# Prompt attention with a third pair of probability buffers

## The chip, the cores and the metric
One core of a Trainium2 chip runs the whole program: one decoder layer for a prompt of 1024 tokens and for 8 sequences of 4 new tokens each. The metric is the device time of one execution in microseconds (us). Engines: PE is TensorE (PEld its weight loads), DVE is VectorE, ACT is ScalarE, POOL is GpSimd, SP is SyncE, which issues most DMAs. Every engine has a queue of its own; what one needs of another it waits for by semaphore.

## The reference, cut to what matters
The layer normalises, projects, runs attention beside a gated convolution, projects out, and then runs a mixture of experts and a gated embedding. The part that the change touches is the attention of the prompt. For each of 8 heads it mixes three dilation patterns, weighted by their softmax denominators, which is one softmax over all keys with a bias that counts each distance as often as a pattern holds it:

```
s   = einsum('bdnqhc,bdnkhc->bdnhqk', qb, kb) * HEAD_DIM**-0.5 + bias
s   = where(valid, s, NEG)
mx  = max(s);  e = exp(s - mx);  den = sum(e)
num = einsum('bdnhqk,bdnkhc->bdnqhc', e, vb)
...
wts = exp(mxs - max(mxs))
out = sum(wts * nums) / sum(wts * dens)
```

The kernel computes for each head and each block of 128 queries the scores against all earlier keys, adds a bias table that holds the log of the counts and the mask, and takes one softmax.

## The kernel before, in words
All arithmetic is float32. In the prompt attention two heads make a pair (four pairs), and each pair takes eight steps, one for each block i of 128 query rows, in the order i = 7, 0, 6, 1, 5, 2, 4, 3 (STEPS, line 139). Step i has 128 (i + 1) keys, so heavy and light steps alternate. In what follows n counts all 32 steps and hh is the head of the pair.

A step passes through these operations. PE: `score(n)` (line 1552), both heads, into PSUM banks 0 to 3, one group of banks for each head, so the next score waits until both were read. DVE: `bias(n, hh)` (L1092) adds the table Z to the scores, writes the result to the probability buffer E and its negated maximum to `nmax`. ACT: `exp(n, hh)` (L796), in place, with its sum in `den`. DVE: `normalise(n, hh)` (L1099 the reciprocal, L1101 the scaling in place). PE: `trans_p(n)` (L1566) turns the i + 1 blocks of each head with the identity, up to four blocks to a PSUM bank, with two banks (4 and 5) in turn; a bank is used again once ACT has copied it out. ACT: `evac_pt(n, hh)` (L807) does that copy into the buffer PTb, of which there are two pairs. PE: `weigh(n)` (L1579) multiplies the values V with the turned probabilities into bank 6 or 7. DVE: `evac_o(n)` (L1106) copies the output to aT. When all eight steps of a pair have been copied, POOL squares, sums and scales that pair's output (lines 615 to 621). E has two pairs of buffers, used by turns; `bias(n)` waits until the transposes of step n - 2 have read theirs.

The order on each engine is written out by hand. PE: score(n), trans_p(n-1), weigh(n-2). ACT: evac_pt(n-1, 0), exp(n, 0), evac_pt(n-1, 1), exp(n, 1). DVE: bias(n, 0), bias(n, 1), evac_o(n-3), normalise(n, 0), normalise(n, 1). SP loads the next pairs' tables Z after counts of the semaphore `scored`, and the first caches for the sample attention after the last one. The sample attention begins on PE, ACT and DVE behind the last step of this stage; its later loads wait for semaphores that hang on the stage's end.

Of the kernel before, what the change touches and what calls it, by code (L numbers as in the profile page):

```python
# [26 lines left out]
ALU = mybir.AluOpType  # L27
ACT = mybir.ActivationFunctionType
AX = mybir.AxisListType

P = 128
D = 1024
SEQ = 1024
# [106 lines left out]
NSTEP = len(STEPS)  # L140


def tp_uses(n):

    return sum(2 * -(-(i + 1) // 4) for _, i in STEPS[:n])
# [37 lines left out]
def build(nc, I, O):  # L183
    ctx = ExitStack()
    with ctx, nc.allow_non_contiguous_dma(reason="gains and router weights, a few KB"):
        _build(nc, I, O, ctx)


def _build(nc, I, O, ctx):
    sem_cache = {}  # L190

    def S(name):
        if name not in sem_cache:
            sem_cache[name] = ctx.enter_context(nc.semaphore(name))
        return sem_cache[name]

    def sb(name, n, dt=F32):
        return ctx.enter_context(nc.sbuf_tensor(name, [P, n], dt))
# [8 lines left out]
    def view(region, at, *dims):  # L207
        n = int(np.prod(dims))
        v = region[:, at:at + n]
        if len(dims) == 2:  # L210
            v = v.rearrange("p (a b) -> p a b", a=dims[0])
        if len(dims) == 3:
            v = v.rearrange("p (a b c) -> p a b c", a=dims[0], b=dims[1])
        return v

    ident = sb("ident", P)
# [12 lines left out]
    small = sb("small", 320)  # L229
    qts = view(sb("qts", NG * SAMP), 0, NG, SAMP)  # L230
    kts = view(sb("kts", NG * SAMP), 0, NG, SAMP)
    R1 = sb("R1", 26880)
    R2 = sb("R2", 12880)
    R3 = sb("R3", 4224)
    R4 = sb("R4", 6144)
# [31 lines left out]
    a_sum = view(R1, 13312, SEQ)  # L267
    Z = [view(R1, 16384 + 1024 * s, SEQ) for s in range(4)]
    aT = view(R1, 22656, CC, TOK)
    E = [[view(R4, 2048 * p + 1024 * hh, SEQ) for hh in range(2)] for p in range(2)]  # L270
    PTb = [[view(r, at + 1024 * hh, PT, P) for hh in range(2)] for r, at in ((R4, 4096), (R1, 20480))]

    near = [view(r, at, NG, NEAR) for r, at in ((R2, 0), (R2, 3584), (R2, 8192), (R1, 20480))]
# [67 lines left out]

    ssx, ms_x, rs_x = small[:, 0:2], small[:, 2:4], small[:, 4:6]
    hd_s, hd_r, hd_q = small[:, 6:22], small[:, 22:38], small[:, 38:54]
    nmax, den, rden = small[:, 54:58], small[:, 58:62], small[:, 62:66]
    ssc, rc = small[:, 88:97], small[:, 97:106]
    nms, dens, rdens = small[:, 106:107], small[:, 107:108], small[:, 108:109]
    ssa, ra = small[:, 140:149], small[:, 150:159]
# [5 lines left out]
    bank = [ctx.enter_context(nc.psum_tensor(f"pair{i}", [P, 1024], F32)) for i in range(4)]  # L353
    bk = [bank[i // 2][:, 512 * (i % 2):512 * (i % 2) + 512] for i in range(8)]
# [353 lines left out]
    def _(act):  # L708
# [82 lines left out]

        def exp(n, hh):
            w = P * (STEPS[n][1] + 1)
            k = 2 * (n % 2) + hh
            act.wait_ge(S("scored"), 2 * n + hh + 1)
            act.activation(E[n % 2][hh][:, 0:w], E[n % 2][hh][:, 0:w], ACT.Exp, bias=nmax[:, k:k + 1],  # L796
                           scale=-1.0, accum_out=den[:, k:k + 1]).then_inc(S("exp_done"), 1)

        def evac_pt(n, hh):
            i = STEPS[n][1]  # L800
            use = tp_uses(n) + hh * (-(-(i + 1) // 4))
            if n >= 2:
                act.wait_ge(S("ot_full"), n - 1)
            for j0 in range(0, i + 1, 4):
                m = min(4, i + 1 - j0)
                act.wait_ge(S("tp_full"), use + 1)
                act.activation(PTb[n % 2][hh][:, j0:j0 + m, :], bk[4 + use % 2].rearrange("p (a b) -> p a b", b=P)[:, 0:m, ::-1],  # L807
                               ACT.Copy).then_inc(S("tp_free"), 1)
                use += 1

        act.wait_ge(S("new_out"), 32)
        for n in range(NSTEP):
            if n >= 1:
                evac_pt(n - 1, 0)
            exp(n, 0)
            if n >= 1:
                evac_pt(n - 1, 1)
            exp(n, 1)
        evac_pt(NSTEP - 1, 0)
        evac_pt(NSTEP - 1, 1)  # L820


        def evac_near(b):
# [140 lines left out]
    def _(dve):  # L964
# [62 lines left out]
        for q in range(CC):  # L1027
# [23 lines left out]
            for j in range(3):  # L1051
                w = wj[:, j, q:q + 1]
# [31 lines left out]
        def bias(n, hh):  # L1084
            pair, i = STEPS[n]
            w = P * (i + 1)
            k = 2 * (n % 2) + hh
            dve.wait_ge(S(f"w_in{2 * (pair % 2) + hh}"), W_DONE[2 * (pair % 2) + hh] + 16 * (pair // 2 + 1))
            dve.wait_ge(S("s_full"), 2 * n + hh + 1)
            if n >= 2:  # L1090
                dve.wait_ge(S("tp_full"), tp_uses(n - 1))
            dve.tensor_tensor_reduce(E[n % 2][hh][:, 0:w], bank[hh][:, 0:w], Z[2 * (pair % 2) + hh][:, SEQ - w:SEQ], -1.0, 3e38,  # L1092
                                     ALU.add, ALU.min, nmax[:, k:k + 1]).then_inc(S("scored"), 1)

        def normalise(n, hh):
            w = P * (STEPS[n][1] + 1)
            k = 2 * (n % 2) + hh
            dve.wait_ge(S("exp_done"), 2 * n + hh + 1)
            dve.reciprocal(rden[:, k:k + 1], den[:, k:k + 1]).then_inc(S("rden"), 1)  # L1099
            dve.wait_ge(S("rden"), 2 * n + hh + 1)  # L1100
            dve.tensor_scalar(E[n % 2][hh][:, 0:w], E[n % 2][hh][:, 0:w], rden[:, k:k + 1], None, ALU.mult).then_inc(S("p_ready"), 1)  # L1101

        def evac_o(n):
            pair, i = STEPS[n]
            dve.wait_ge(S("ot_full"), n + 1)
            dve.tensor_copy(aT[:, pair, P * i:P * i + P], bk[6 + n % 2][:, 0:P]).then_inc(S("ot_free"), 1)  # L1106

        for n in range(NSTEP):
            bias(n, 0)
            bias(n, 1)  # L1110
            if n >= 3:
                evac_o(n - 3)
            normalise(n, 0)
            normalise(n, 1)
        for n in range(NSTEP - 3, NSTEP):
            evac_o(n)


# [310 lines left out]
    def _(pe):  # L1429
# [9 lines left out]
        for q in range(CC):  # L1439
            last = pe.transpose(bk[7][:, 16 * q:16 * q + 16], st_in[:, P * q:P * q + P], ident[0:16, 0:16])  # L1440
# [68 lines left out]
        for q in range(CC):  # L1509
            pe.wait_ge(S(f"kv_in{q % 2}"), 16 * (q // 2 + 1))  # L1510
            for j, (lo, n) in enumerate(PIECES):
                use = 3 * q + j
                for which, full, b in ((2, "cC_full", use % 2), (0, "ch_full", 2 + use % 2), (1, "cB_full", 4 + j)):
# [10 lines left out]
                    for c in range(DC):  # L1524
                        last = mm(bk[b][:, 0:n], wB[q % 2][:, c, which, :], xT[:, c, lo:lo + n], start=(c == 0), stop=(c == DC - 1))  # L1525
# [3 lines left out]
        for q in range(CC):  # L1529
            last = pe.transpose(bk[0][0:18, P * q:P * q + P], u_new[:, 18 * q:18 * q + 18], ident[:, :])  # L1530
        last.then_inc(S("new_full"), 1)
        pe.wait_ge(S("y_sum"), CC)
        for t in range(TILES):
            n = P if t < PT else SAMP
            last = mm(bk[7][0:n, t:t + 1], y_sum[:, P * t:P * t + n], ones[:, 0:1], start=True, stop=True)
# [7 lines left out]
        def score(n):  # L1543
            pair, i = STEPS[n]
            w = P * (i + 1)
            if n >= 1:
                pe.wait_ge(S("scored"), 2 * n)
            for c0 in range(0, w, 512):
                m = min(512, w - c0)
                for hh in range(2):  # L1550
                    half = slice(64 * hh, 64 * hh + 64)
                    last = mm(bank[hh][:, c0:c0 + m], QT[half, pair, P * i:P * i + P], KT[half, pair, c0:c0 + m], start=True, stop=True)  # L1552
                    if c0 + m == w:
                        last.then_inc(S("s_full"), 1)

        def trans_p(n):
            i = STEPS[n][1]
            use = tp_uses(n)
            for hh in range(2):
                pe.wait_ge(S("p_ready"), 2 * n + hh + 1)  # L1560
                for j0 in range(0, i + 1, 4):
                    m = min(4, i + 1 - j0)
                    if use >= 2:
                        pe.wait_ge(S("tp_free"), use - 1)
                    for j in range(m):
                        last = pe.transpose(bk[4 + use % 2][:, P * j:P * j + P], E[n % 2][hh][:, P * (j0 + j):P * (j0 + j) + P], ident[:, :])  # L1566
                    last.then_inc(S("tp_full"), 1)
                    use += 1

        def weigh(n):  # L1570
            pair, i = STEPS[n]
            pe.wait_ge(S("tp_free"), tp_uses(n + 1))
            if n >= 2:
                pe.wait_ge(S("ot_free"), n - 1)
            for j in range(i + 1):
                for hh in range(2):
                    half = slice(64 * hh, 64 * hh + 64)
                    c = DH * (2 * pair + hh)
                    last = mm(bk[6 + n % 2][half, 0:P], V[:, j, c:c + DH], PTb[n % 2][hh][:, j, :], start=(j == 0), stop=(j == i))  # L1579
            last.then_inc(S("ot_full"), 1)  # L1580

        for n in range(NSTEP):
            score(n)
            if n >= 1:
                trans_p(n - 1)
            if n >= 2:
                weigh(n - 2)
        trans_p(NSTEP - 1)
        weigh(NSTEP - 2)
        weigh(NSTEP - 1)  # L1590
# [77 lines left out]
        for t in range(PT):  # L1668
            last = mm(bk[7][:, t:t + 1], a_sum[:, P * t:P * t + P], ones[:, 0:1], start=True, stop=True)
# [18 lines left out]
        for q in range(CC):  # L1688
            last = mm(bk[4][0:SAMP, 0:1], as_sq[:, q, :], ones[:, 0:1], start=(q == 0), stop=(q == CC - 1))
# [230 lines left out]
```

## Time and profile before
| | |
|---|---|
| median of 3 runs | 1448.4 us (1447.89 to 1451.6) |
| profiled execution | 1454.46 us, its span 1452.4 us |
| PE busy, share of the span | 1262.4 us, 87% |
| DVE, ACT, POOL busy | 403.7, 320.8, 168.5 us |
| granted TensorE clock, mean of the span | 0.931 |
| prompt attention, 403.5 to 556 us | PE busy 126.03, DVE 107.31, ACT 95.55 of 152.50 us, clock 0.90 |

The busy time says how much of the span an engine worked, the chain of waits says which work ended last, and the timeline gives each instruction's start and length. The granted clock is 1.00 at 2.4 GHz and 0.50 at 1.2 GHz. The start of one instruction to the start of the next is the better price of PE's work, since the ends of matmuls are modelled.

### The profile page before, as it was taken

Reading aid. Unit: us, or ns where it says so; the run is one execution under the profiler, and the core shown is the slowest. Engines: PE = TensorE matmul, PEld = TensorE weight load, DVE = VectorE, ACT = ScalarE, POOL = GpSimd, SP = SyncE. Lnnn points to the kernel's source line nnn. Section 1 sums busy time; section 2 is a strip of 40 time slices with the busy share of each in tenths; the row PEclk is TensorE's granted clock in tenths of the full one; section 3 lists DMA queues with packets and bytes.
Section 4 is the critical chain, followed back from the end, with each engine's and each line's share of the span. In section 5 each row is a group of like instructions: output and inputs, shape, how many; then the busy total and the mean of one; then the engine's idle time right before and its main releaser. Section 6 shows DMA issues by size and latency. Waiting matters only on the chain.

```text
span 1452.4 us, 16889 instructions
## 1 busy us (share of the span) xinstructions
PE 1262.4 (87%) x6484; PEld 816.4 (56%) x6484; DVE 403.7 (28%) x829; ACT 320.8 (22%) x625; POOL 168.5 (12%) x222
## 2 busy tenths in 40 slices
PE   4999999999978887567999407999999999789995
PEld 1444445666555557243555307888888888534442
DVE  1121221122257775121322531111111111033332
ACT  2132321000057664130111200111111111123332
POOL 0000000000031221000000052222222221100000
PEclk9999999999979998787999758999999999979998
DMA  7111400130040005898111422888888888432210
GB/s 260 36 51 43 119 15 19 44 102 0 27 127 31 30 1 162 202 267 301 73 73 47 191 89 64 308 308 294 310 297 322 317 318 327 189 129 90 86 50 33
DMA packets 64453, 208.84 MB, mean 144 GB/s; under 512 B 16158, under 2 KB 29758, under 8 KB 48528
## 3 DMA queue, kind: packets, MB, share of 16 engines
q1 hardware_dynamic: 50704, 177.61, 35.6%
q0 software_dynamic: 13696, 30.49, 5.8%
q8 instruction: 37, 0.61, 0.2%
q14 instruction: 16, 0.13, 0.0%
HBM read 194.43 MB, written 29.89 MB: 154 GB/s over the span
## 4 chain that ended last, share of the span: by engine, by line
PE 81%; DMA 6%; DVE 6%; issue 3%; ACT 2%; POOL 1%; SPq 1%; POOLq 0%; ACTq 0%; DVEq 0%
PE pair L1778 17%; PE pair L1473 12%; PE pair L1525 11%; PE pair L1710 8%; PE pair L1877 8%; PE pair L1788 8%; DMA R<-in_cache_v 4%; PE pair L1552 3%; PE pair L1566 2%; PE pair L1769 2%; PE pair L1859 2%; PE pair L1579 2%; DVE R L1101 1%; PE pair L1603 1%; POOL list_dram L640 1%
## 5 line engine op out<-in xcount | busy, mean ns | idle before, releaser
L1778 PEld LDWEIGHTS pair<-R 128*128 128x128 f32 x2048 | 247.6, 197 | 16.5 <-issue 14.2
L1778 PE MATMUL pair<-R 128*128 128x128 f32 x2048 | 247.9, 282 | 1.7 <-DVE R L1357 1.7
L1525 PE MATMUL pair<-R 128*128 128x352 f32 x576 | 172.5, 463 | 0.4 <-ACT kts L758 0.4
L1473 PE MATMUL pair<-R 128*128 128x512 f32 x384 | 170.6, 601 | 0.8 <-DVE R L993 0.8
L1525 PEld LDWEIGHTS pair<-R 128*128 128x128 f32 x576 | 110.2, 192 | 61.8 <-issue 1.4
L1473 PEld LDWEIGHTS pair<-R 128*128 128x128 f32 x384 | 72.9, 193 | 87.8 <-issue 86.6
L1788 PE MATMUL pair<-R,bias_s 128*128 128x512 f32 x256 | 115.3, 593 | 1.4 <-DVE bias_s L1363 1.4
L1710 PE MATMUL pair<-R 128*128 128x512 f32 x256 | 114.6, 602 | 0.0
L1877 PE MATMUL pair<-R 128*128 128x512 f32 x256 | 112.9, 599 | 0.8 <-ACT R L932 0.8
L1357 DVE COPY R<-pair 128x512 f32<-128x512 f32 x64 | 41.3, 686 | 238.2 <-PE pair L1769 238.2
L1877 PEld LDWEIGHTS pair<-R 128*128 128x128 f32 x256 | 49.2, 193 | 62.9 <-issue 62.9
L898 ACT ACTIVATE R<-pair 128x512 f32<-128x512 f32 x32 | 19.1, 597 | 292.4 <-PE pair L1788 292.4
L1710 PEld LDWEIGHTS pair<-R 128*128 128x128 f32 x256 | 48.3, 193 | 55.6 <-issue 55.6
L1769 PE MATMUL pair<-ident,R 128*128 128x128 f32 x256 | 34.3, 278 | 45.8 <-DMA R<-m_dram,idx_c 45.8
L1788 PEld LDWEIGHTS pair<-R,bias_s 128*128 128x128 f32 x256 | 46.2, 190 | 48.2 <-issue 45.9
L1566 PE MATMUL pair<-ident,R 128*128 128x128 f32 x288 | 46.3, 302 | 22.1 <-DVE R L1101 16.2
L1769 PEld LDWEIGHTS pair<-ident,R 128*128 128x128 f32 x256 | 31.5, 189 | 46.6 <-issue 46.6
L1566 PEld LDWEIGHTS pair<-ident,R 128*128 128x128 f32 x288 | 34.0, 151 | 40.6 <-DVE R L1101 36.2
L807 ACT ACTIVATE R<-pair 128x512 f32<-128x512 f32 (+3 forms) x96 | 43.8, 484 | 43.3 <-PE pair L1566 43.0
L796 ACT ACTIVATE R<-R,small 128x1024 f32<-128x1024 f32 (+7 forms) x64 | 49.4, 772 | 6.0 <-DVE small L1092 5.5
L1092 DVE CUSTOM_DVE_ANT_0 R<-pair,R 128x1024 f32<-128x1024 f32 (+7 forms) x64 | 45.8, 753 | 13.8 <-PE pair L1552 13.7
L1552 PE MATMUL pair<-R 64*128 64x512 f32 (+3 forms) x192 | 44.6, 573 | 4.1 <-DVE small L1092 3.5
(266 smaller groups left out, 1172.0 us busy)
## 6 DMA issues: line engine op xcount, KB each, us to landing
R<-in_w_gate SPq DMA_DIRECT2D x32, 1024.0 KB, 7.3
R<-in_w_up SPq DMA_DIRECT2D x32, 1024.0 KB, 9.7
R<-in_w_down SPq DMA_DIRECT2D x32, 1024.0 KB, 12.9
R<-in_x_prompt SPq DMA_DIRECT2D x16, 512.0 KB, 3.5
R<-in_cache_k SPq DMA_DIRECT2D x8, 1024.0 KB, 7.8
R<-in_cache_v SPq DMA_DIRECT2D x8, 1024.0 KB, 19.7
R<-y_dram SPq DMA_DIRECT2D x16, 512.0 KB, 4.3
R<-in_w_in SPq DMA_DIRECT2D x3, 2048.0 KB, 10.3
```

The costliest lines, as they stand in the source:

```text
L796: act.activation(E[n % 2][hh][:, 0:w], E[n % 2][hh][:, 0:w], ACT.Exp, bias=nmax[:, k:k + 1], scale=-1.0, accum_out=den[:, k:k + 1]).then_i ...
L807: act.activation(PTb[n % 2][hh][:, j0:j0 + m, :], bk[4 + use % 2].rearrange("p (a b) -> p a b", b=P)[:, 0:m, ::-1], ACT.Copy).then_inc(S(" ...
L1092: dve.tensor_tensor_reduce(E[n % 2][hh][:, 0:w], bank[hh][:, 0:w], Z[2 * (pair % 2) + hh][:, SEQ - w:SEQ], -1.0, 3e38, ALU.add, ALU.min, n ...
L1473: last = mm(bk[4 + part][0:n, :], xTs[a.u][:, c, 0:n], wA[:, c, AD * part:AD * part + AD], start=(c == 0), stop=(c == DC - 1))
L1525: last = mm(bk[b][:, 0:n], wB[q % 2][:, c, which, :], xT[:, c, lo:lo + n], start=(c == 0), stop=(c == DC - 1))
L1552: last = mm(bank[hh][:, c0:c0 + m], QT[half, pair, P * i:P * i + P], KT[half, pair, c0:c0 + m], start=True, stop=True)
L1566: last = pe.transpose(bk[4 + use % 2][:, P * j:P * j + P], E[n % 2][hh][:, P * (j0 + j):P * (j0 + j) + P], ident[:, :])
L1710: last = mm(bk[2 * pair + j][0:n, :], lhs[:, q, P * a.t:P * a.t + P], w_out[:, c0 + q, 512 * j:512 * j + 512], start=(q == 0), stop=(q == ...
L1769: last = pe.transpose(bk[j][:, CAP * (c % 4):CAP * (c % 4) + CAP], xg[u][:, c:D:DC], ident[0:CAP, 0:CAP])
L1778: last = mm(bk[2 + u][:, CAP * (2 * side + j):CAP * (2 * side + j) + CAP], w[:, c, j:FE:2], xgT[u][:, c, :], start=(c == 0), stop=(c == DC ...
L1788: last = mm(bk[4 + 2 * u + j][0:CAP, :], hT[u][:, q, :], wd[s][:, q, 512 * j:512 * j + 512], start=(q == 0), stop=(q == 1))
L1877: last = mm(bk[2 + j][0:n, :], hnT[a.u][:, c, 0:n], w_pg[c][:, 512 * j:512 * j + 512], start=(c == 0), stop=(c == DC - 1))
```

## The change
A third pair of buffers for E is placed in region R1 at 14336, `nmax`, `den` and `rden` have six columns instead of four, and E is used by n % 3. PE transposes step n - 2 and weighs step n - 3 behind score(n). ACT runs exp(n, 0), evac_pt(n-2, 0), exp(n, 1), evac_pt(n-2, 1). DVE runs both bias operations of n, then the scaling of n - 1, then the output copy of n - 4. `bias(n)` waits for the transposes of step n - 3. The buffers PTb and all PSUM banks stay as they were.

```diff
-    E = [[view(R4, 2048 * p + 1024 * hh, SEQ) for hh in range(2)] for p in range(2)]
+    E = [[view(r, at + 1024 * hh, SEQ) for hh in range(2)] for r, at in ((R4, 0), (R4, 2048), (R1, 14336))]
...
-    nmax, den, rden = small[:, 54:58], small[:, 58:62], small[:, 62:66]
+    nmax, den, rden = small[:, 54:60], small[:, 60:66], small[:, 66:72]
...
         act.wait_ge(S("new_out"), 32)
         for n in range(NSTEP):
-            if n >= 1:
-                evac_pt(n - 1, 0)
             exp(n, 0)
-            if n >= 1:
-                evac_pt(n - 1, 1)
+            if n >= 2:
+                evac_pt(n - 2, 0)
             exp(n, 1)
-        evac_pt(NSTEP - 1, 0)
-        evac_pt(NSTEP - 1, 1)
+            if n >= 2:
+                evac_pt(n - 2, 1)
+        for n in range(NSTEP - 2, NSTEP):
+            evac_pt(n, 0)
+            evac_pt(n, 1)
...
-            if n >= 2:
-                dve.wait_ge(S("tp_full"), tp_uses(n - 1))
+            if n >= 3:
+                dve.wait_ge(S("tp_full"), tp_uses(n - 2))
...
             bias(n, 0)
             bias(n, 1)
-            if n >= 3:
-                evac_o(n - 3)
-            normalise(n, 0)
-            normalise(n, 1)
-        for n in range(NSTEP - 3, NSTEP):
+            if n >= 1:
+                normalise(n - 1, 0)
+                normalise(n - 1, 1)
+            if n >= 4:
+                evac_o(n - 4)
+        normalise(NSTEP - 1, 0)
+        normalise(NSTEP - 1, 1)
+        for n in range(NSTEP - 4, NSTEP):
             evac_o(n)
...
             score(n)
-            if n >= 1:
-                trans_p(n - 1)
             if n >= 2:
-                weigh(n - 2)
+                trans_p(n - 2)
+            if n >= 3:
+                weigh(n - 3)
+        trans_p(NSTEP - 2)
+        weigh(NSTEP - 3)
         trans_p(NSTEP - 1)
         weigh(NSTEP - 2)
         weigh(NSTEP - 1)
```
The remaining lines of the diff put n % 3 for n % 2 where E, `nmax`, `den` and `rden` are indexed.

## Rows read from the trace of the kernel before

**Rows 1.** Windows: us, PE, PEld, DVE, ACT, POOL busy, granted clock, DMA share, GB/s
```profile
487.00:524.00 37.00, 31.29 (x270) 21.07 (x268) 27.19 (x73) 23.28 (x56) 7.60 (x3) 0.91 0.01 1
```

**Rows 2.** Chain that ended last, in order: start us, us, what
```profile
441.43 1.97 PE pair L1552 x8
...
475.29 1.97 PE pair L1552 x8
...
512.19 1.97 PE pair L1552 x8
...
545.38 1.06 PE pair L1552 x4
...
553.65 0.29 DVE R L1106
```

**Rows 3.** Who waited for whom, 419 to 553 us: total us, times, longest
```profile
PEld pair L1566 <- DVE R L1101: 33.0, 35, 2.4
```

**Rows 4.** Timeline from step i = 6: start, us, instruction, idle before and its releaser
```profile
450.68 1.77 PE L1552 MATMUL pair<-R 64*128 64x512 f32 x8
...
452.38 0.44 PE L1566 MATMUL pair<-ident,R 128*128 128x128 f32 x2
452.58 1.10 DVE L1092 CUSTOM_DVE_ANT_0 R<-pair,R 128x896 f32<-128x896 f32 x1 [1.21 <-PE pair L1552]
452.75 1.73 PEld L1579 LDWEIGHTS pair<-R 128*64 128x64 f32 x32 [0.17 <-issue]
...
453.72 1.04 ACT L796 ACTIVATE R<-R,small 128x896 f32<-128x896 f32 x1 [0.63 <-DVE small L1092]
...
454.76 0.26 ACT L807 ACTIVATE R<-pair 128x128 f32<-128x128 f32 x1
```

**Rows 5.** Timeline: an evacuation and the transposes that it lets go
```profile
424.30 0.98 ACT L807 ACTIVATE R<-pair 128x512 f32<-128x512 f32 x2 [0.54 <-PE pair L1566]
...
425.04 0.96 PE L1566 MATMUL pair<-ident,R 128*128 128x128 f32 x7 [0.51 <-ACT R L807]
```

**Rows 6.** Timeline of the steps with i = 4 and i = 7
```profile
433.78 1.35 PE L1552 MATMUL pair<-R 64*128 64x512 f32 x8
...
435.06 0.88 PE L1566 MATMUL pair<-ident,R 128*128 128x128 f32 x6
...
436.95 0.47 ACT L807 ACTIVATE R<-pair 128x384 f32<-128x384 f32 x1
...
441.36 1.99 PE L1552 MATMUL pair<-R 64*128 64x512 f32 x8
...
443.27 1.09 PE L1566 MATMUL pair<-ident,R 128*128 128x128 f32 x8
...
445.88 0.58 ACT L807 ACTIVATE R<-pair 128x512 f32<-128x512 f32 x1
```

**Rows 7.** Timeline: the score of step 1
```profile
409.94 0.80 PE L1552 MATMUL pair<-R 64*128 64x128 f32 x4 [2.59 <-DVE small L1092]
```

**Rows 8.** Timeline: POOL's work for a pair and the scaling beside it
```profile
454.98 1.89 POOL L615 TENSOR_TENSOR R<-R 128x1024 f32<-128x1024 f32 x1 [41.89 <-DVE R L1106]
455.08 2.27 DVE L1101 TENSOR_SCALAR R<-R,small 128x896 f32<-128x896 f32 x1
...
457.46 1.36 DVE L1101 TENSOR_SCALAR R<-R,small 128x896 f32<-128x896 f32 x1
...
491.32 2.59 DVE L1101 TENSOR_SCALAR R<-R,small 128x896 f32<-128x896 f32 x1
```

**Rows 9.** Timeline of PE's pauses; windows of PE: us, busy, granted clock
```profile
457.41 0.98 PE L1566 MATMUL pair<-ident,R 128*128 128x128 f32 x7 [1.96 <-DVE R L1101]
...
528.17 1.37 PE L1566 MATMUL pair<-ident,R 128*128 128x128 f32 x7 [1.96 <-DVE R L1101]
...
491.00:491.10 0.10, 0.00 (x0) 0.89 0.00 0
497.90:498.00 0.10, 0.10 (x2) 0.98 0.00 0
```

More of the change, by code:

```diff
@@ L793, in exp @@
             w = P * (STEPS[n][1] + 1)
-            k = 2 * (n % 2) + hh
+            k = 2 * (n % 3) + hh
             act.wait_ge(S("scored"), 2 * n + hh + 1)
-            act.activation(E[n % 2][hh][:, 0:w], E[n % 2][hh][:, 0:w], ACT.Exp, bias=nmax[:, k:k + 1],
+            act.activation(E[n % 3][hh][:, 0:w], E[n % 3][hh][:, 0:w], ACT.Exp, bias=nmax[:, k:k + 1],
                            scale=-1.0, accum_out=den[:, k:k + 1]).then_inc(S("exp_done"), 1)
@@ L1086, in bias @@
             w = P * (i + 1)
-            k = 2 * (n % 2) + hh
+            k = 2 * (n % 3) + hh
             dve.wait_ge(S(f"w_in{2 * (pair % 2) + hh}"), W_DONE[2 * (pair % 2) + hh] + 16 * (pair // 2 + 1))
             dve.wait_ge(S("s_full"), 2 * n + hh + 1)
-            if n >= 2:
-                dve.wait_ge(S("tp_full"), tp_uses(n - 1))
-            dve.tensor_tensor_reduce(E[n % 2][hh][:, 0:w], bank[hh][:, 0:w], Z[2 * (pair % 2) + hh][:, SEQ - w:SEQ], -1.0, 3e38,
+            if n >= 3:
+                dve.wait_ge(S("tp_full"), tp_uses(n - 2))
+            dve.tensor_tensor_reduce(E[n % 3][hh][:, 0:w], bank[hh][:, 0:w], Z[2 * (pair % 2) + hh][:, SEQ - w:SEQ], -1.0, 3e38,
                                      ALU.add, ALU.min, nmax[:, k:k + 1]).then_inc(S("scored"), 1)
@@ L1096, in normalise @@
             w = P * (STEPS[n][1] + 1)
-            k = 2 * (n % 2) + hh
+            k = 2 * (n % 3) + hh
             dve.wait_ge(S("exp_done"), 2 * n + hh + 1)
@@ L1100, in normalise @@
             dve.wait_ge(S("rden"), 2 * n + hh + 1)
-            dve.tensor_scalar(E[n % 2][hh][:, 0:w], E[n % 2][hh][:, 0:w], rden[:, k:k + 1], None, ALU.mult).then_inc(S("p_ready"), 1)
+            dve.tensor_scalar(E[n % 3][hh][:, 0:w], E[n % 3][hh][:, 0:w], rden[:, k:k + 1], None, ALU.mult).then_inc(S("p_ready"), 1)
         def evac_o(n):
@@ L1565, in trans_p @@
                     for j in range(m):
-                        last = pe.transpose(bk[4 + use % 2][:, P * j:P * j + P], E[n % 2][hh][:, P * (j0 + j):P * (j0 + j) + P], ident[:, :])
+                        last = pe.transpose(bk[4 + use % 2][:, P * j:P * j + P], E[n % 3][hh][:, P * (j0 + j):P * (j0 + j) + P], ident[:, :])
                     last.then_inc(S("tp_full"), 1)
```

## The prediction

> **What bounds the kernel now.** I read the stage's windows first, then the chain that ended last, then who waited for whom, then the timeline of single steps. The windows show that the stage belongs to PE: in a 37 us stretch PE is busy for 31.3 us [rows 1], DVE and ACT for less. The chain gives the period of a head pair (eight steps): the 128-row blocks i = 7, 0, 6, 1, 5, 2, 4, 3. It passes the first score of pairs 1, 2 and 3 at 441.43, 475.29 and 512.19 us, the last score at 545.38 and the last output copy at 553.65 [rows 2]. So the periods are 33.86 and 36.90 us, and the stage, which begins at about 403.5, takes 150 us. In the waits the largest one of PE in this stage is for the scaling of the probabilities (L1101): 33.0 us over 35 times on the weight-load side [rows 3]. That is the wait which the change aims at: a transpose stands one step behind its score, and the step's exp and scaling are not done when PE comes to it. After the stage the sample attention waits for its end by the same semaphores as before, so whatever the stage gains or loses I take to the end of the kernel one for one.
>
> **The change, part by part.** With a distance of two steps every p_ready is long there: the scaling of step n-2 ends before PE has finished step n-1. This removes the waits of rows 3. What is late next is the question, and it is in ACT's order. Before: evacuate first half of n-1, exp(n,0), evacuate second half, exp(n,1). After: exp(n,0), evacuate first half of n-2, exp(n,1), evacuate second half. The transposes use two PSUM banks (up to four blocks each), and every half of a step with i of 4 or more fills both. So the second half's first transpose needs an evacuation that now stands behind exp(n,0), which needs bias(n,0), which needs the score that PE has only just made. And because heavy (i = 7, 6, 5, 4) and light steps alternate, n and n-2 are both heavy: before, the heavy transposes stood beside a light exp.
>
> Price of that wait, from the step with i = 6: score starts 450.68, bias 452.58, exp 453.72, ACT free for the next one 454.76 [rows 4], that is 4.08 us after the score began. From the start of an evacuation to the transpose that it lets go is 0.74 us (424.30 to 425.04) [rows 5]. So PE can start the second half 4.82 us into the step. It gets there earlier: score 1.70 us (to 452.38) [rows 4] and eight transposes at 0.107 us (0.86 for eight, the busy 1.09 of rows 6 being modelled past its hand-over) make 2.56. Pause: 2.26 us. In the same way i = 7: 4.52 + 0.74 = 5.26 against 1.91 + 0.54 (the block it turns is i = 4 of the pair before, five transposes) = 2.45, pause 2.81; i = 4: 3.17 + 0.74 = 3.91 against 1.28 + 0.64 = 1.92, pause 1.99 [rows 6]; i = 5 lies between: 4.36 against 2.24, pause 2.12. Together 9.2 us of pauses in each pair. The light steps have none: one bank for each half, both free by then.
>
> PE's own work in a pair: 72 transposes at 0.107 and 8 hand-overs of 0.17 are 9.0 us; 144 weighting matmuls at 0.054 (1.73 us for 32) [rows 4] and 8 hand-overs are 9.1; the scores are 1.91 + 1.70 + 1.49 + 1.28 for the heavy and about 2.9 for the light ones, 9.3. Sum 27.4 us, with the pauses 36.6. Against that the before has 33.86 and 36.90 [rows 2]: 6.5 and 9.5 above the same work. The longer of the two holds things that I price below.
>
> What the change saves beside rows 3: when a pair ends, GpSimd squares and scales its output (454.98), and the scaling on DVE takes 2.27 us beside it and 2.59 in the later pairs, where GpSimd has one more multiply, against 1.36 for the same shape only partly beside it [rows 8]. PE waits for both. Afterwards GpSimd starts some 5 us later in the pair, at the output copy which now follows the scaling, and what it blocks is a light step's scaling that PE needs a step later: hidden, at most 2.6 us a pair if the cover were gone. The bias operation itself ran at its usual length beside GpSimd.
>
> Start and end. Before, the third score stood behind the first step's transposes. It can now start once bias(1) is done: score 1 runs from 409.94 for 0.80 us [rows 7], then 0.2, two short biases and 0.14, so at 411.6. Steps 2 to 7 are then scores of 7.0, 1.7 more for the first of them at the lower clock, transposes of steps 0 to 5 of 6.7, weightings of steps 0 to 4 of 6.0 and three pauses of 6.4: 27.8, so the next pair begins at 439.4 instead of 441.43: -2.1 us. Pairs 1 to 3 up to the last score: 3 x 36.6 less the last step's 3.3 (score 1.06, transposes 0.81, weighting 1.46) = 106.5 against 545.38 - 441.43 = 103.95: +2.5. After the last score one more transpose step and one more weighting are left (2.3 us of work), less 0.9 of the 1.6 us that PE now waits in those 8.27: +1.4. The wider nmax/den/rden, the third buffer's place and the queue of SP (its table loads wait for counts of scored, as before) cost nothing; that engine idles here. Sum without the clock: -2.1 + 2.5 + 1.4 = +1.8 us.
>
> **The clock.** PE's pauses of 1.96 us, three in this stage (the first and the last in rows 9), came from the blocked scaling. The first left the granted clock at 2.4 GHz, the other two were each followed by 1.2 GHz, the middle one from 491.1 to 497.9, that is 6.8 us [rows 9]. A spell costs at least what the two periods differ by, less the longer second scaling: 3.04 - (2.59 - 1.36) = 1.8 us [rows 2, 8]; at most half of 6.8, 3.4 us, if PE has no pause in it to hide behind. After the change there are 15 pauses of 1.99 to 2.81 us (three in pair 0, four in each other), each at least as long as those that tipped the clock two times in three. I take six in ten: 9 spells, at 2.2 us, nearer the measured price: 20 us. (The two spells of before are in its periods already, and its 1.96 us pauses are gone.) Bounds: none, 0, and all at the high price, 51.
>
> Forecast: +1.8 + 20 = +22 us on the profiled execution's 1454.5. That execution is 6 us above the median of 1448.4; I put the difference on the median: 1470 us.
>
> **A rule of the skill.** The trace shows ACT's exp and evacuations in program order only, in every step of rows 4 to 6. The Trainium skill, page "TensorE: Matmul & The Clock Gate", section on the architectural detail of the array, says that ScalarE and VectorE are strict first-in first-out queues and only TensorE may pull something ahead, its weight loads. By that rule, which speaks against this change, the evacuation cannot pass the waiting exp and the sum stays +22; if it could, the first rival below would hold.
>
> **Rivals.**
> A, faster. The second half's bank is free in time, because exp(n,0) and the evacuation come sooner than I add up. Then PE runs its 27.4 us per pair: 3 x 27.4 - 3.3 = 78.9 against 103.95 is -25, with start and end -26: 1423 us. For it: DVE has slack, so every bias can start the moment its score ends, and the change does take away rows 3. Against it: even then bias and exp of the same step lie between, 2.18 us (452.58 to 454.76) for i = 6. It decides from pauses under about 1.5 us in each heavy step (6.5 a pair, as before): there the kernel begins to be faster.
> B, no change. The pauses are there and the clock stays at 2.4 GHz through them, as after the first of rows 9: +1.8, 1450 us.
> C, slower still: every pause is followed by a spell at the high price: +53, 1501 us.
> D, the trade is only moved: GpSimd's block lands on a scaling that PE needs at once, up to 2.6 us in three pairs, +8 on B: 1458 us. Against it: a full step lies between.
>
> **How the numbers follow.** Forecast (some spells, +6 to +40, so 1454 to 1488) 0.66, A 0.09, B 0.14, C 0.06, D 0.05. The range 1449 to 1490 leaves A and C out. About 0.3%, 4.3 us, is what a measurement of this kernel can tell from no change. Faster is A and a little of B's spread: 0.10. Within: most of B, 0.12. Slower: the rest, 0.78.
>
> **What would show it.** Right: PE's waits for L1101 nearly gone; in their place waits of the transposes (L1566) for ACT's evacuation (L807), four in a pair and of 2 to 2.8 us; ACT waiting for bias (L1092) rather than for PE; periods of 36.6 us or more; several spells at 1.2 GHz in the stage, and a mean granted clock there well under the 0.91 of rows 1; GpSimd's block without a pause of PE behind it. Wrong: periods near 28 us or pauses under 1.5 us (A); pauses as priced with the clock at 2.4 GHz (B). If the time moves while the stage from 403.5 to 554 us keeps its length, the cause is elsewhere and the whole argument fails.

## The result, and the profile after

| kernel | runs | median, us | lowest to highest |
|---|---|---|---|
| before | 4 | 1448.44 | 1447.89 to 1451.60 |
| after | 4 | 1461.04 | 1459.76 to 1465.62 |

The change makes the kernel slower: ratio 1.0094, 95% interval 1.0078 to 1.0111, which is +12.6 us. 1470 was forecast, the sign and the place were right, the size was too large.

The profiled execution of after took 1459.76 us. In its chain of waits the scores and the copies stand as follows (start us, us, what); the rows answer to [rows 2]:

```profile
476.15 0.69 PE pair L1556 x3
...
515.65 0.70 PE pair L1556 x3
...
553.23 1.11 PE pair L1556 x4
...
562.78 0.29 DVE R L1107
```
From its timeline, the first score of pairs 1, 2 and 3:

```profile
436.57 1.99 PE L1556 MATMUL pair<-R 64*128 64x512 f32 x8
...
476.08 1.99 PE L1556 MATMUL pair<-R 64*128 64x512 f32 x8
...
515.58 1.99 PE L1556 MATMUL pair<-R 64*128 64x512 f32 x8
```
The periods are 39.51 and 39.50 us, where before had 33.86 and 36.90. Line numbers moved: L1556 is the score, L1570 the transposes, L1583 the weighting, L1093 the bias, L1100 and L1102 the reciprocal and the scaling, L1107 the output copy. From the score of step 1 to the last output copy the stage took 157.6 us (405.20 to 562.78); before it took 143.7 (409.94 to 553.65). That is +13.9, and it agrees with the medians. The profiled spans differ by 5.3 only, since the stage began 4.7 us earlier in this execution and the sample attention behind it was 4 us shorter. Both vary as much between executions of kernels that are alike there (from the last output copy to the first matmul of the output projection the profiles have 115.0 to 128.9 us), so I compare the stage.

Who waited for whom, from 413 to 562 us of after (total us, times, longest), answering to [rows 3]:

```profile
ACT R L796 <- DVE small L1093: 62.4, 28, 4.0
...
PEld pair L1570 <- DVE R L1102: 29.6, 16, 2.8
PE pair L1570 <- ACT R L807: 25.2, 16, 2.6
...
PE pair L1570 <- DVE R L1102: 5.4, 3, 2.0
...
ACT R L807 <- PE pair L1570: 1.8, 4, 0.7
```
ACT now waits for bias, no longer for the transposes, and PE waits for ACT's evacuations. In before (419 to 553 us) ACT's row was:

```profile
ACT R L807 <- PE pair L1566: 40.1, 33, 2.7
```
The row of PEld looks as if nothing had changed since [rows 3] (33.0 us there). It names the wrong releaser, as the next rows and e1_evac_first show. The timeline of a step with i = 6, answering to [rows 4], shows the pause:

```profile
487.06 1.77 PE L1556 MATMUL pair<-R 64*128 64x512 f32 x8
488.76 1.09 PE L1570 MATMUL pair<-ident,R 128*128 128x128 f32 x8
488.96 1.09 DVE L1093 CUSTOM_DVE_ANT_0 R<-pair,R 128x896 f32<-128x896 f32 x1 [2.90 <-issue]
...
490.09 1.04 ACT L796 ACTIVATE R<-R,small 128x896 f32<-128x896 f32 x1 [4.00 <-DVE small L1093]
...
491.13 1.06 ACT L807 ACTIVATE R<-pair 128x512 f32<-128x512 f32 x2
...
491.85 1.06 PE L1570 MATMUL pair<-ident,R 128*128 128x128 f32 x8 [2.00 <-DVE R L1102]
```
The second half's transposes start 4.79 us after the score, 0.72 us after the evacuation. The releaser that the last row names, the scaling at L1102, is the wrong one. The scaling with which DVE was busy just then is of another step (n-1) and one block wide, and PE needs it a step later. A releaser is inferred from semaphore events, and where two come close together their times have to be read against the program's order.

### The profile page after: what moved, and what is told of

It is laid out like the page before. It is cut to its first block, busy times and chain, and to the rows that moved or that the text cites. A ratio compares the mean times of both kernels' runs of the same rounds, so it can differ in the third digit from the quotient of the medians.

```text
span 1457.7 us, 16889 instructions
## 1 busy us (share of the span) xinstructions
PE 1259.4 (86%) x6484; PEld 817.3 (56%) x6484; DVE 393.3 (27%) x829; ACT 316.7 (22%) x625; POOL 166.6 (11%) x222
## 3 DMA queue, kind: packets, MB, share of 16 engines
q1 hardware_dynamic: 50704, 177.61, 35.4%
## 4 chain that ended last, share of the span: by engine, by line
PE 80%; DMA 6%; issue 5%; DVE 4%; ACT 2%; POOL 1%; SPq 1%; POOLq 0%; DVEq 0%; ACTq 0%
PE pair L1784 17%; PE pair L1477 11%; PE pair L1529 11%; PE pair L1716 8%; PE pair L1883 8%; PE pair L1794 8%; DMA R<-in_cache_v 4%; PE pair L1583 3%; PE pair L1570 2%; PE pair L1556 2%; PE pair L1775 2%; PE pair L1865 2%; PE pair L1609 1%; POOL list_dram L640 1%; PE pair L1743 1%
## 5 line engine op out<-in xcount | busy, mean ns | idle before, releaser
L1570 PE MATMUL pair<-ident,R 128*128 128x128 f32 x288 | 47.4, 306 | 30.6 <-ACT R L807 25.2
L1093 DVE CUSTOM_DVE_ANT_0 R<-pair,R 128x1024 f32<-128x1024 f32 (+7 forms) x64 | 46.0, 756 | 63.0 <-PE pair L1556 41.7
L1570 PEld LDWEIGHTS pair<-ident,R 128*128 128x128 f32 x288 | 34.9, 154 | 50.0 <-DVE R L1102 30.7
L1556 PE MATMUL pair<-R 64*128 64x512 f32 (+3 forms) x192 | 46.1, 590 | 3.8 <-DVE small L1093 3.3
L1367 DVE TENSOR_TENSOR bias_s<-pair,R 128x256 f32<-128x256 f32 x32 | 13.6, 424 | 115.2 <-ACT R L895 115.2
```

The costliest lines, as they stand in the source:

```text
L1093: dve.tensor_tensor_reduce(E[n % 3][hh][:, 0:w], bank[hh][:, 0:w], Z[2 * (pair % 2) + hh][:, SEQ - w:SEQ], -1.0, 3e38, ALU.add, ALU.min, n ...
```

## The experiments

The "stage" below is, as above, from the score of step 1 to the last output copy in each profiled execution.

| kernel | stage, us | median, us | ratio to before, 95% |
|---|---|---|---|
| before | 143.7 | 1448.4 | |
| after | 157.6 | 1461.0 | 1.0078 to 1.0111 |
| e1_evac_first | 126.0 | 1430.0 | 0.9858 to 0.9900 |
| e2_both_evacs_first | 125.3 | 1435.6 | 0.9876 to 0.9940 |
| e3_filled_pauses | 145.4 | 1449.6 | 0.9989 to 1.0024 |
| e4_before_exp_first | 180.2 | 1486.3 | 1.0251 to 1.0318 |
| e5_evac_first_weigh_between | 125.1 | 1430.6 | 0.9848 to 0.9905 |
| e6_weigh_between | 144.5 | 1449.1 | 0.9987 to 1.0028 |
| e7_before_no_pool | 135.7 | 1439.5 | 0.9932 to 0.9967 |
| e8_heavy_beside_light | - | 1454.0 | 1.0019 to 1.0058 |

The medians of before in the three later comparisons were 1447.75 (e1 to e4), 1447.81 (e5 to e7) and 1449.07 (e8).

**e1_evac_first: ACT's order put back.**

```diff
         for n in range(NSTEP):
-            exp(n, 0)
             if n >= 2:
                 evac_pt(n - 2, 0)
-            exp(n, 1)
+            exp(n, 0)
             if n >= 2:
                 evac_pt(n - 2, 1)
+            exp(n, 1)
```


> The changed kernel with ACT's order as before the change: evacuation of the first half of n-2, exp(n,0), evacuation of the second half, exp(n,1). If the pauses come from the evacuation queued behind exp(n,0), each heavy step's 2.0 to 2.6 us pause of PE shrinks to some 0.3 us, a pair takes 28 to 30 us instead of 39.5, the 1.2 GHz spells in the stage go, and the time is 1422 to 1432 us, under both kernels. Rival: the pauses come from DVE's scaling (the trace names L1102 at the steps with i = 6): then they stay and the time is 1456 to 1462.

1430 us, 31 below after and 18 below before. The timeline of the step with i = 6:

```profile
439.41 1.77 PE L1556 MATMUL pair<-R 64*128 64x512 f32 x8
...
441.11 1.09 PE L1570 MATMUL pair<-ident,R 128*128 128x128 f32 x8
...
441.87 1.09 ACT L807 ACTIVATE R<-pair 128x512 f32<-128x512 f32 x2 [1.84 <-PE pair L1570]
...
442.61 1.06 PE L1570 MATMUL pair<-ident,R 128*128 128x128 f32 x8 [0.40 <-ACT R L807]
442.84 1.04 ACT L796 ACTIVATE R<-R,small 128x896 f32<-128x896 f32 x1
```
The evacuation runs as soon as the transposes are there, PE's pause is 0.40 us instead of 2.00, and the exp comes 0.4 us later than it could, for which nobody waits. From 413 to 531 us the clock stays at 2.4 GHz. PEld's row, 29.6 us in after, has all but gone, although no line of DVE was changed:

```profile
PEld pair L1570 <- DVE R L1102: 4.3, 6, 1.0
```
The pair took 30.5 us (expected: 28 to 30), the next 31.5. The 1.0 us between them is GpSimd's longer block, which now delays a scaling of two blocks that PE needs:

```profile
484.36 0.44 PE L1570 MATMUL pair<-ident,R 128*128 128x128 f32 x2 [0.77 <-DVE R L1102]
```
All of the difference between a loss of 13 us and a gain of 18 is this order on ACT. The rival, that DVE's scaling was the releaser, fell.

**e2_both_evacs_first.** As e1, with both evacuations ahead of both exps:

```diff
             if n >= 2:
                 evac_pt(n - 2, 0)
-            exp(n, 0)
-            if n >= 2:
                 evac_pt(n - 2, 1)
+            exp(n, 0)
             exp(n, 1)
```


> As the last one, but both evacuations stand before both exps. If only the evacuation of the first half matters, this is within 3 us of it, since nobody waits for an exp until a step later. If exps are now late for the scaling, PE waits for L1102 again and it is 5 us or more slower than that kernel.

Its median lies 5.6 us above that of e1, outside the 3 us, but the intervals overlap and the stage is as short (125.3 against 126.0). PE waited 2.3 us for the scaling in both, so the reason given for a slower e2 is not in the trace. In its profiled execution, at 1441.0 us, the sample attention behind the stage took 128.9 us, in that of e1 119.6. Whether that is chance I did not settle; e2's runs spread from 1426.0 to 1443.4.

**e3_filled_pauses: the clock's share by itself.** In after, in each pause:

```diff
             for hh in range(2):
+                if hh == 1 and i >= 4 and n < NSTEP - 2:
+                    if n >= 3:
+                        pe.wait_ge(S("ot_free"), n - 2)
+                    for _ in range({4: 22, 5: 16, 6: 17, 7: 18}[i]):
+                        pe.transpose(bk[6 + (n - 1) % 2][:, 256:256 + P], ident[:, :], ident[:, :])
                 pe.wait_ge(S("p_ready"), 2 * n + hh + 1)
```


> The changed kernel with 16 to 22 idle transposes of the identity into an unused part of the next output bank, in each of the 15 pauses (1.7 to 2.35 us of work, 0.2 to 0.4 less than the pause): nothing waits for them and no wait is taken away. If the spells at 1.2 GHz are the second part of the loss, they go and the time falls by 10 to 13 us to 1448 to 1451, with periods of 36.6 us. If the spells cost nothing because PE waits for ACT anyway, the time stays at 1461, or rises by what the added work costs.

1449.6 us, 11.4 below after although PE does more. Its timeline, and its windows of PE (us, busy, granted clock):

```profile
446.62 1.77 PE L1556 MATMUL pair<-R 64*128 64x512 f32 x8
448.32 1.09 PE L1575 MATMUL pair<-ident,R 128*128 128x128 f32 x8
449.25 2.13 PE L1568 MATMUL pair<-ident 128*128 128x128 f32 x18
451.42 1.06 PE L1575 MATMUL pair<-ident,R 128*128 128x128 f32 x8
```
```profile
437.00:474.00 37.00, 36.78 (x345) 1.00 0.10 31
474.00:510.00 36.00, 35.78 (x337) 1.00 0.09 30
```
The second half starts 4.80 us after the score, as in after, so the pause is as long; it is only filled. The clock stays at 2.4 GHz and the periods are 36.42 and 36.43 us. After's own 39.5 hold two spells at 1.2 GHz each:

```profile
480.00:490.00 10.00, 8.53 (x65) 0.83 0.00 0
490.00:500.00 10.00, 8.15 (x72) 0.83 0.01 2
500.00:510.00 10.00, 7.29 (x68) 1.00 0.01 2
...
520.00:530.00 10.00, 9.17 (x60) 0.66 0.01 2
```
A spell of 3.4 us is a clock of 0.83 over 10 us; the one at 520 lasted twice as long. So after minus before is made of two parts: the pauses, with what the change saves already taken off (before's own two spells too), +1.9 us (e3 against before on the same chip), and the clock, 11.4 us by the medians and 12.6 by the two ratios to before.

**e4_before_exp_first.** ACT's new order in the kernel before, at distance one:

```diff
-            if n >= 1:
-                evac_pt(n - 1, 0)
             exp(n, 0)
             if n >= 1:
-                evac_pt(n - 1, 1)
+                evac_pt(n - 1, 0)
             exp(n, 1)
+            if n >= 1:
+                evac_pt(n - 1, 1)
```


> The kernel before with ACT's order alone changed, exp(n,hh) ahead of the evacuation of n-1. At distance one a heavy step's transposes stand beside a light exp (0.4 to 0.7 us), so the delay should be small: 1448 to 1454 us. Rival: the order alone costs what the whole change costs, at any distance: 1459 to 1463.

Both were wrong: 1486 us, 38 above before and far more than the whole change costs. I had counted only the length of the light exp. The timeline of a light step (i = 1) shows the rest:

```profile
461.97 0.70 PE L1552 MATMUL pair<-R 64*128 64x256 f32 x4
...
464.63 1.73 PE L1566 MATMUL pair<-ident,R 128*128 128x128 f32 x7 [1.96 <-DVE R L1101]
464.68 1.35 DVE L1101 TENSOR_SCALAR R<-R,small 128x896 f32<-128x896 f32 x1
465.95 0.41 DVE L1092 CUSTOM_DVE_ANT_0 R<-pair,R 128x256 f32<-128x256 f32 x1
...
466.41 0.51 ACT L796 ACTIVATE R<-R,small 128x256 f32<-128x256 f32 x1 [2.99 <-DVE small L1092]
...
466.92 0.96 ACT L807 ACTIVATE R<-pair 128x512 f32<-128x512 f32 x2
...
467.64 1.73 PE L1566 MATMUL pair<-ident,R 128*128 128x128 f32 x7 [1.28 <-DVE R L1101]
```
At distance one, bias(n) stands on DVE behind both scalings of n-1, so the evacuation waits for exp, exp for bias, and bias for the scaling: the first half turned at 464.63, its bank came free only after 466.92. That this is the whole of the 38 us is read from the trace, not tested.

**e5_evac_first_weigh_between.** e1, and on PE the weighting between the two halves (`trans_p` is told which half to turn):

```diff
...
             if n >= 2:
-                trans_p(n - 2)
+                trans_p(n - 2, (0,))
             if n >= 3:
                 weigh(n - 3)
+            if n >= 2:
+                trans_p(n - 2, (1,))
```


> The changed kernel with ACT's order as in e1_evac_first, and on PE the weighting of n-3 between the two halves of the transposes of n-2. In e1_evac_first a pair took 30.5 us against 27.4 of PE's work; if what is left are the short waits for a bank between the halves, real work now covers them: 28 to 29 us a pair, 1422 to 1427 us. If the rest is work that I priced too low, the time stays at 1430.

No gain: 30.4 us for a pair, 31.2 for the next, and 1430.6 us. The short waits between the halves were not the last bound. Another shows in their place at i = 7:

```profile
435.02 1.99 PE L1556 MATMUL pair<-R 64*128 64x512 f32 x8
...
439.57 0.49 PE L1556 MATMUL pair<-R 64*128 64x128 f32 x4 [0.36 <-DVE small L1093]
```
The next score waits for both bias operations of this one, since each head has one set of score banks: 4.55 us from score to score, against 3.95 of PE's work.

**e6_weigh_between.** Only that PE order, with exp still first on ACT (the same edit, made in after).

> The changed kernel with exp still first on ACT, and only PE's order as in the last one: in a heavy step the light weighting (0.4 to 1.0 us) covers part of the pause. By the theory a pair loses 2.8 us of pauses (0.37 + 0.59 + 0.81 + 1.03) and, the pauses being 1.2 to 2.0 us, most of the spells at 1.2 GHz: 1442 to 1450 us. If any exp ahead of the evacuation costs the full 2 us whatever PE does meanwhile, it stays at 1458 to 1462.

1449.1 us, 12 below after, inside the expected 1442 to 1450. With real work in part of the pause the pairs took 35.4 and 36.9 us, and two spells were left (from 477.9 and 515.4 us, 3.4 us each) of after's seven. So the loss depends on what PE does meanwhile, and an order on PE mends what the order on ACT costs, but only a part.

**e7_before_no_pool.**

```diff
         for pair in range(NG):
             pool.wait_ge(S("ot_free"), 8 * (pair + 1))
-            rows = aT[:, pair, 0:SEQ]
+            c = 2 if pair in (1, 2) else SEQ
+            rows = aT[:, pair, 0:c]
...
```


> The kernel before, with GpSimd's squaring, summing and scaling of pairs 1 and 2 cut to two columns each (left out for the rest: the output of the attention is not the reference's). It prices what the change hides. By the prediction's sum the two periods with the long block lose 3.5 us of blocked scaling and a 1.8 us spell each, so the stage is 10 to 11 us shorter and the time about 1437. If DVE's longer scaling is not GpSimd's doing, or is hidden, the stage keeps its 143.7 us.

The stage lost 8.0 us instead of 10 to 11, the time 8.3. The first scores of pairs 1, 2 and 3:

```profile
437.04 1.99 PE L1553 MATMUL pair<-R 64*128 64x512 f32 x8
...
470.90 1.99 PE L1553 MATMUL pair<-R 64*128 64x512 f32 x8
...
503.17 1.99 PE L1553 MATMUL pair<-R 64*128 64x512 f32 x8
```
With pair 0's block still there the period is 33.86 as in [rows 2], without a block 32.27. So before's 36.90 held 4.6 us of GpSimd's long block and its spell. One spell of 3.4 us stayed in pair 3 (510.7 to 514.1), with no long block beside it and behind waits of only 0.29, 0.63 and 0.52 us. By half its length, an estimate, it can account for at most 1.7 of the 2.6 us that are missing. This block is what the change hides.

**e8_heavy_beside_light.** In after, the order of the blocks:

```diff
-STEPS = [(pair, i) for pair in range(NG) for i in (7, 0, 6, 1, 5, 2, 4, 3)]
+STEPS = [(pair, i) for pair in range(NG) for i in (7, 6, 0, 1, 5, 4, 2, 3)]
```


> The changed kernel with one size changed: the order of the blocks in a pair is 7, 6, 0, 1, 5, 4, 2, 3, so that a heavy step is turned beside the exp of a light one. By the theory the pauses shrink with the exp and bias that stand before the evacuation: i = 7 turned in the step of 0 waits 0.8 us, 6 in that of 1 1.2, 5 in that of 2 1.5, 4 in that of 3 1.9, 5.3 instead of 9.2 a pair; two heavy scores in a row now wait for the bias of each other, some 2 us a pair. So 34.5 to 35 us a pair without spells, fewer spells, and 1440 to 1450 us. If the order of heavy and light does not matter, and any exp ahead costs the same, the time stays at 1459 to 1463.

1454 us, 7 below after (8 by the ratios to before) but above the expected 1440 to 1450. The pauses shrank as worked out: those for i = 6, 5 and 4 stand in the trace as 0.9, 1.45 and 1.6 us, and the one for i = 7 is split into waits of 0.37, 0.62 and 0.30 us. PE's waits for the bias of the score just before it took 1.8 us a pair. But each of the last three pairs still had a spell, and their periods were 37.5 and 37.8 us. From the first score to the last output copy the stage took 156.8 us, after's 163.9, which is the 7 us of the medians. Heavy beside heavy makes the loss larger; it is not its cause. The spells did not follow the longest pauses that were left. They began at 453.7, 491.3 and 528.8 us, each among the short waits at i = 7, while the clock stayed up behind the pauses of 1.45 and 1.6 us:

```profile
451.20 0.49 PE L1556 MATMUL pair<-R 64*128 64x128 f32 x4 [0.46 <-DVE small L1093]
452.07 0.66 PE L1570 MATMUL pair<-ident,R 128*128 128x128 f32 x4 [0.37 <-DVE R L1102]
453.35 0.79 PE L1570 MATMUL pair<-ident,R 128*128 128x128 f32 x4 [0.62 <-ACT R L807]
```

## Why the prediction was right in kind and too large

**The wait that takes the place of the one removed: right.** Priced at 4.82 us from score to second half for i = 6, measured 4.79 and 4.80. The pauses, priced 2.81, 2.26, 2.12 and 1.99, stand in the trace as 2.56, 2.00, 1.87 and 1.74, all 0.25 less, because the end of the matmul before is modelled later than the hand-over from which I counted; the first pause of the stage, at 413 us, was 1.40. Rival A, that exp and evacuation come soon enough, needed pauses under 1.5 us: it fell, and e1 shows what it would have been worth (1430, where A said 1423).

**PE's work and the period: right.** 36.6 us a pair without spells, measured 36.42 in e3. From the first score of pair 1 to the last score, 106.5 forecast, 105.95 in e3 (437.20 to 543.15).

**Start and end: right.** The step from the last score to the last copy grew from 8.27 to 9.6 us (+1.4 forecast). Step 1 to pair 1 took 29.8 us in e3 against 31.4 before: -1.6, where -2.1 was forecast.

**The sum without the clock: right.** +1.8 forecast; e3 less before is +1.9, interval -1.6 to +3.5 us. Rival B was a fair account of this part, but the clock did not stay up.

**GpSimd's block: right.** It starts later in the pair and hits a light step's scaling. After's timeline, to be held against [rows 8]:

```profile
498.46 1.89 POOL L617 TENSOR_TENSOR R<-R 128x1024 f32<-128x1024 f32 x1 [34.33 <-DVE R L1107]
...
501.94 1.00 DVE L1102 TENSOR_SCALAR R<-R,small 128x256 f32<-128x256 f32 x1
...
503.04 1.10 DVE L1102 TENSOR_SCALAR R<-R,small 128x256 f32<-128x256 f32 x1
```
PE took up that block at 504.74, straight behind the score: hidden. Rival D fell. The cover is the pauses themselves: without them, in e1, the same block costs 1.0 us in each of the last two pairs. Two details of [rows 8] were read wrongly, without weight for the sum. The extra operation of the later pairs is an add, not a multiply, and the scaling of 1.36 us ran wholly, not partly, beside GpSimd's scaling (456.85 to 460.06); with GpSimd idle the same shape took 0.69 us (422.81 in before).

**The clock: the step that failed, in size.** The forecast's term was 9 spells at 2.2 us, 20 us. Measured were 7 spells in the stage, and 11.4 to 12.6 us (after less e3; 12.2 by the stages): 1.6 to 1.8 us for a spell, no more than my lower bound of 1.8. Six of the seven lasted 3.4 us; only the one from 520.5 to 527.3 lasted the 6.8 of [rows 9], from which both ends of my price were taken. Together the seven are 27.3 us at 1.2 GHz. An estimate from that is a cost of at most half, 13.7 us, and the measured one lies somewhat below. The count was off as well. One chance for every pause was the wrong form: in pairs 1 to 3 the clock fell at each of the six pauses of 2.00 and 2.56 us (between 0.3 us before their end and 1.6 us after it), and at one of the other nine. Why most spells were shorter is read from the rows and not tested. In before, the blocked scaling of the second half made another pause inside the spell (0.94 us, to 493.96); in after, PE has more than 5 us of nearly uninterrupted work behind each pause. But the spell at 520.5 had such work behind it too, and lasted 6.8. So I took the length from a place with a different neighbourhood, and what decides it stays open. Rival C was further off on both counts. The mean granted clock was no good sign either: 0.89 over the stage against 0.92 before, not "well under".

**The rule of the Trainium skill: the trace and e1 agree.** The rule is the one that the prediction took from the page "TensorE: Matmul & The Clock Gate", section on the architectural detail of the array, that ScalarE keeps its queue in order. ACT never took an evacuation ahead of the exp that stood before it, though its input lay ready for 1.6 us (transposes at 488.76, evacuation at 491.13, against 0.76 us between the two in e1), and putting it first in program order gained 31 us.

**What I did not ask.** The forecast compared the change with before, and did not price its nearest neighbour, the same distance with ACT's old order. By the same sum, with pauses of 0.3 to 0.6 us, it was in reach: a pair of 29 us. The change's idea is worth 18 us; one swap in its ACT loop spent 31.

## What to carry to other kernels

When a pipeline is made one step deeper, write down for each in-order queue what each instruction now stands behind, above all those that free a buffer: an evacuation goes ahead of work whose input is only just being made. A second stage of distance removes the wait for data, and the wait for space (two PSUM banks here, one set of score banks in e5) is next. Price a pause of PE twice, once as time and once as a possible fall of the clock, and take the length of such a spell from a place with the same work behind it. Count short waits that stand close together too: in e7 and e8 the clock fell at waits of at most 0.63 us.

## What the runs showed of the hardware that I had not expected

Filling a pause with transposes of the identity that nobody needs made the kernel 11.4 us faster: 15 pauses of at most 2.6 us had lowered the clock seven times. The length of a single pause does not foretell it: in before one of 1.96 us left the clock up, and in e8 pauses of 1.6 us did, while a row of waits of at most 0.63 us brought it down in each of e8's last three pairs and once in e7. In after PE worked almost without a break behind each fall, and the spell lasted 3.4 us in six cases of seven; in before, where another pause came soon, 6.8 in both cases. Ahead of the stage, executions differ by up to 5 us although nothing is changed there: its first score began at 398.8 to 403.8 us in these profiles, so two profiled spans alone could not have sized this change.
